# The first layer's beginning put in another order: loads, network rounds, modulation chunks, row norms, filter evacuation, angle tables

## The reference, cut to what matters

```
mod  = silu(c) @ ada_w[l] + ada_b[l]          # 6 x 1024: sh1 sc1 g1 sh2 sc2 g2
h    = rms_norm(x, ln1_g[l]) * (1 + sc1) + sh1
cols = h @ w_in[l]                            # four column groups a, b, c, d
y_d  = hyena(cols_d, filters)                 # filters: below, by FFT
x    = x + g1 * (concat(y_a, y_b, y_c, y_d) @ w_out[l])
x    = x + g2 * hier_moe(rms_norm(x, ln2_g[l]) * (1 + sc2) + sh2)

# filters: sine network of three rounds, then a product with w4 and a decay window
h = sin(f0 * (z @ w1 + b1)); h = sin(f1 * (h @ w2 + b2)); h = sin(f2 * (h @ w3 + b3))
h = (h @ w4) * window ; filt = two-sided(h) * rsqrt(sum(filt^2) + eps) ; F = rfft(filt)
# rope: cos and sin of positions * inv_freq, used by groups a, b and c
```

## Time and profile before

| | |
|---|---|
| median of three executions | 1690.1 us (1688.35 to 1690.55) |
| the profiled execution: its time | 1678.52 us |
| its span, first to last instruction | 1676.7 us |
| PE busy | 1373.4 us, 82% of the span |
| VectorE busy | 617.6 us, 37% |
| mean granted clock of TensorE | 0.929 of full |

### The profile page before, as it was taken

One profiled execution on the slowest core, in us unless ns is written; L12 is line 12 of the kernel. 1 busy time (PEld: TensorE's weight loads), 2 busy tenths in 40 slices (PEclk: granted clock), 3 DMA queues, 4 the chain that ended last, 5 costly groups with the idle time before them and its releaser, 6 DMA issues.

```text
span 1676.7 us, 18442 instructions
## 1 busy us (share of the span) xinstructions
PE 1373.4 (82%) x6748; PEld 775.2 (46%) x6748; DVE 617.6 (37%) x1444; ACT 370.6 (22%) x835; POOL 269.2 (16%) x250
## 2 busy tenths in 40 slices
PE   2779999898969589888988999998869779987731
PEld 0244655565544245444444564565544345544420
DVE  3462523256733511333153342246761432111111
ACT  0221112445521111111202112344540211111101
POOL 0000210000000053332220120000000124333211
PEclk9779999999989699999988999999989879999986
DMA  7621021267243789999943122234033669999933
GB/s 234 250 77 40 11 93 74 89 231 249 90 174 126 277 300 315 408 407 404 373 166 107 50 91 76 75 144 173 13 131 130 263 232 326 402 400 404 393 125 113
DMA packets 98608, 336.75 MB, mean 201 GB/s; under 512 B 28370, under 2 KB 33106, under 8 KB 73272
## 3 DMA queue, kind: packets, MB, share of 16 engines
q1 hardware_dynamic: 74712, 305.52, 46.7%
q0 software_dynamic: 15072, 16.85, 4.5%
q10 hardware_dynamic: 8736, 13.21, 2.2%
HBM read 324.08 MB, written 28.98 MB: 211 GB/s over the span
## 4 chain that ended last, share of the span: by engine, by line
PE 67%; DVE 14%; ACT 7%; issue 5%; DMA 3%; POOL 2%; SPq 1%; POOLq 0%; DVEq 0%; ACTq 0%
PE bank L493 62%; ACT pr_r L1333 2%; PE bank L747 2%; PE bank L842 2%; DVE pr_r L1963 2%; DVE pr_r L1822 1%; ACT pr_r L1380 1%; DVE pr_r L1966 1%; DMA big<-in_ada_w_dram 1%; DVE pr_r L1685 1%; POOL small L1451 1%; PE bank L597 1%; SPq L985 1%; ACT ht_r L1312 1%; DVE small L1820 1%
## 5 line engine op out<-in xcount | busy, mean ns | idle before, releaser
L493 PE MATMUL bank<-big,pr_r 128*64 128x256 f32 (+2 forms) x3192 | 451.8, 402 | 65.1 <-issue 25.1
L493 PEld LDWEIGHTS bank<-big,pr_r 128*64 128x64 f32 (+1 forms) x3192 | 269.3, 152 | 218.8 <-issue 108.7
L493 PE MATMUL bank<-big,ht_r 128*128 128x512 f32 (+2 forms) x832 | 330.1, 548 | 1.5 <-ACT ht_r L1346 1.5
L493 PEld LDWEIGHTS bank<-big,ht_r 128*128 128x128 f32 x832 | 155.0, 190 | 145.2 <-issue 137.6
L493 PE MATMUL bank<-big 128*128 128x256 f32 (+4 forms) x496 | 175.5, 492 | 27.9 <-ACT big L1317 10.5
L1516 POOL DMA_INDIRECT x_rows<-ht_r,slot_i x64 | 101.8, 1591 | 324.8 <-DVE ht_r L1969 289.0
L493 PEld LDWEIGHTS bank<-big 128*128 128x128 f32 (+2 forms) x496 | 94.4, 202 | 78.1 <-issue 34.2
L1963 DVE TENSOR_TENSOR pr_r<-pr_r,bank 64x256 f32<-64x256 f32 x65 | 27.5, 423 | 247.5 <-ACT pr_r L1380 236.1
L1380 ACT ACTIVATE pr_r<-bank 64x256 f32<-64x256 f32 x64 | 24.1, 377 | 408.5 <-PE bank L493 408.5
L1450 POOL TENSOR_SCALAR small<-small 128x1 f32<-128x1 f32 (+2 forms) x20 | 7.9, 396 | 561.3 <-DVE small L1847 334.0
L1969 DVE SCALAR_TENSOR_TENSOR ht_r<-bank,mix_r,mod 128x512 f32<-128x512 f32 x65 | 48.8, 751 | 132.6 <-PE bank L493 132.6
(11 more groups left out here) (296 smaller groups left out, 1254.5 us busy)
## 6 DMA issues: line engine op xcount, KB each, us to landing
big<-in_moe_w_gate_dram SPq DMA_DIRECT2D x63, 1024.0 KB, 15.7
big<-in_moe_w_up_dram SPq DMA_DIRECT2D x63, 1024.0 KB, 21.4
big<-in_moe_w_down_dram SPq DMA_DIRECT2D x63, 1024.0 KB, 23.9
big<-in_ada_w_dram SPq DMA_DIRECT2D x16, 3072.0 KB, 11.4
big<-in_w_in_dram SPq DMA_DIRECT2D x4, 3072.0 KB, 14.2
big<-in_w_out_dram SPq DMA_DIRECT2D x4, 2048.0 KB, 8.1
mod<-in_ada_b_dram SPq DMA_DIRECT2D x12, 512.0 KB, 9.9
big<-in_w_in_dram SPq DMA_DIRECT2D x2, 2048.0 KB, 8.1
```

Of the source, the lines that this page charges most:

```text
L493: return nc.tensor.matmul(o, l, r, start=start, stop=stop)
```

## The change

It puts layer 0's beginning in another order on all engines; the products and elementwise operations of the program stay the same ones.

- SyncE: `c`, the network's weights and `zT` first, then ada 0, the modulation biases, `w4` and `window`, ada 1, and only then the six other constants. Then, each when its slot or data allow: ada 2, x, the tables of waves, in d, `bias_b`, the vectors of attention, convolution and router, in a.
- PE: `f1` directly behind `f0`, `f2` behind ada 0's products, two filter row tiles ahead of ada 1's, the sums of squares further back. Of the eight DFT products the four of the cosine stay ahead of the projection, with the first transposes between them; the four of the sine go behind `d5`.
- VectorE: the three rounds without `mod_take` between them; rows of x ahead of the filters' evacuation, half of which (`fd`) goes behind the projection d; the small lambda work and the angle tables follow the evacuation of `fc`.
- ScalarE: the angle tables' sines come behind the evacuation of `hT`, as does the exponential of lambda, so its function table is loaded seven times in the program instead of five.
- Semaphores are split (`c_in`, `z_in`, `bias_in`), so that a wait names only what it needs. Scratch buffers move (`s_b_of`, `f_even_of`, `f_odd_of`, `lam_tmp`, `sq_junk`). In layer 1 the products keep their order; the lambda work goes behind its rows.

```
 @block.tensor
-            pe.wait_ge(first_load, 16 * 7)
-            pe.wait_ge(ones_set, 1)
-            pe.wait_ge(rep_ready, 1)
...
-                    pe.wait_ge(net_in, 16 * 7)
-                    pe.wait_ge(hy_in, 16 * 4)
-                    for j, (w, n) in enumerate(((hw1, 33), (hw2, 64), (hw3, 64))):
-                        if j:
-                            pe.wait_ge(mlp_ready, j)
-                        mm(V.bank(f"f{j}")[0:64, :], w, zT if j == 0 else mlp_h).then_inc(ready_v, 1)
-                        if j:
-                            mod_sum(j - 1)
-                        if j < 2:
-                            mod_parts_sum("ada", j)
...
+                    pe.wait_ge(net_in, 16 * 7)
+                    pe.wait_ge(z_in, 16)
+                    network(0)
+                    pe.wait_ge(mlp_ready, 1)
+                    network(1)
+                    pe.wait_ge(rep_ready, 1)
+                    mod_parts_sum("ada", 0)
+                    pe.wait_ge(mlp_ready, 2)
+                    network(2)
+                    pe.wait_ge(ones_set, 1)
+                    mod_sum(0)
+                    pe.wait_ge(mlp_ready, 3)
+                    pe.wait_ge(hy_in, 16 * 2)
+                    filter_rows(0)
+                    filter_rows(1)
+                    mod_parts_sum("ada", 1)
...
 @block.sync
-            load_network(0)
-            load_filters(0)
-            load_chunk(("ada", 0), 0)
-            sp.wait_ge(tables_ready, 1)
-            load_mods(0)
-            load_attention(0)
-            load_conv(0)
-            load_router(0)
-            load_chunk(("ada", 1), 0)
-            for t in range(NT):
-                sp.dma_start(x_tok[:, t, :], a["x"][0, t * P:(t + 1) * P, :]).then_inc(x_in[t], 16)
-            load_waves()
-            load_empty()
+            sp.dma_start(c_sb, a["c"].rearrange("b (p k) -> p (b k)", k=KT)).then_inc(c_in, 16)
+            load_network(0)
+            load_positions()
+            load_chunk(("ada", 0), 0)
+            load_mods(0)
+            load_filters(0)
+            load_chunk(("ada", 1), 0)
+            load_constants()
...
+                    if c == ("in", "a") and l == 0:
+                        load_bias(0)
+                        sp.wait_ge(c_ready, 1)
+                        load_attention(0)
+                        load_conv(0)
+                        load_router(0)
+                        load_empty()
 @block.scalar
-                taken(act, "fdo1")
+                act.wait_ge(nss_ready, 2 * NT * l + NT)
                 for t in range(NT):
                     evac(t)
+                act.wait_ge(lam_pre, l + 1)
+                A_(lexp, lred, ACT.Exp).then_inc(lam_exp, 1)
+                if l == 0:
+                    act.wait_ge(ang_ready, 1)
```

More of the change, by code:

```diff
@@ L554, in layer @@
                     last.then_inc(ready_v, 1)
-                    pe.wait_ge(srep_ready, l + 1)
+                    mod_sum(2)
+                    pe.wait_ge(first_load, 16 * 6)
+                    pe.wait_ge(srep_ready, 1)
                     b = V.bank("fnb")
@@ L1634, in mod_take @@
                         took(last)
-                if l == 0:
-                    v.wait_ge(net_in, 16 * 7)
-                    v.wait_ge(hy_in, 16 * 4)
-                    step(TS(bias_b, bias_b, 2.0 / (2 * S), None, ALU.mult))
-                    for j in range(3):
-                        b = V.take(f"f{j}")
-                        took(TS(mlp_y, b[0:64, :], hb[:, j:j + 1], hf[:, j:j + 1], ALU.add, ALU.mult))
-                        reduce_angle(step, mlp_y, mlp_k).then_inc(sin_in, 1)
-                        if j:
-                            v.wait_ge(mod_in, 16 * 4)
-                            mod_take(j - 1)
-                else:
+                if l:
                     v.wait_ge(mod_in, 16 * 4 * (l + 1))
@@ L1693, in rows, with filter_evac @@
                         last.then_inc(hrow_ready, 1)
-                if l == 0:
+                def filter_evac(kind):
+                    dst = {"c": fc, "d": fd}[kind]
+                    even, odd, scale = f_even_of[l], f_odd_of[l], s_b_of[l]
+                    for m in range(2):
+                        b = V.take(f"f{kind}e{m}")
+                        took(TT(even, b[:, :], scale, ALU.mult))
+                        if kind == "c":
+                            step(TT(even, even, bias_b, ALU.add))
+                        b = V.take(f"f{kind}o{m}")
+                        took(TT(odd, b[:, :], scale, ALU.mult))
+                        TT(dst[:, m, 0], even, odd, ALU.add)
+                        step(TT(dst[:, m, 1], even, odd, ALU.subtract))
@@ L1710, in layer @@
-                for t in range(0 if l else 2, NT):
-                    if t >= 2:
-                        done(v, f"hT{t - 2}1")
-                    rows(t, gsc1, sh1)
+                for t in range(2, NT):
+                    done(v, f"hT{t - 2}1")
+                    rows(t, gsc1, sh1)
+                if l == 0:
+                    v.wait_ge(bias_in, 16)
+                    step(TS(bias_b, bias_b, 2.0 / (2 * S), None, ALU.mult))
+                    filter_evac("c")
+                v.wait_ge(vec_in, 16 * 12 * (l + 1))
```

213 lines of the change are left out of this document (120 added, 93 removed).

## The result

| | before | after |
|---|---|---|
| median | 1689.22 us (1681.28 to 1690.55, 4 executions) | 1643.53 us (1640.46 to 1648.56, 4 executions) |
| profiled execution: time | 1678.52 us | 1640.46 us |
| its span | 1676.7 us | 1638.6 us |
| mean granted clock | 0.929 | 0.938 |
| PE busy | 1373.4 us | 1363.1 us |

The change is faster: ratio 0.9748, 95% interval 0.9725 to 0.9772. The medians lie 45.7 us apart, the two profiled executions 38.1, since the one of before was quick for its kernel.

The account below looks back on a forecast made before the run. Until projection d at 116.94 load and engine waits bound the kernel, then PE's products. Gains of 27.1 and 14.8 (41.9), minus 7.0 handed back, plus 2.3 for clock, gave 37.2: median 1653 us, range 1644 to 1667.

Parts of the forecast that it names:

- First part: Program start until the third sine: reordered loads and an earlier third round end it at 29.0 instead of 56.1, gaining 27.1.
- From 29.0 to `fn`: PE's filter rows, ada 1's products, sums of squares and ada 2's products, forecast to run from 29.0 to 55.6.
- Rival 2: The order works, but PE runs at half clock or ada 1 is late: gain 21 to 32, chance 0.27.
- From `fnb` to the projection: PE's cosine products and transposes beside VectorE's rows: from 58.6, last rows released by transposes, projection d at 75.
- Handed back: The four sine groups, moved behind `d5` where PE is the bound, cost 7.0 of the gain.
- At nothing: Filter evacuation, tables, late vectors, in d, layer 1's lambda work and two more function table loads: covered, costing nothing.
- limit of HBM: A cited page's 358 GB/s for one core would bring ada 1 some 4 us later and cut the gain by that.
- rival 1: The forecast itself: whole kernel gains 32 to 43 us, chance 0.60.
- rival 3: Better than forecast: chunks' products take less than 4.3 and ada 0 comes at 17.3; gain 43 to 47, chance 0.07.
- three signs of failure: Ada 1's products after 40, clock at 0.50 from 30 to 60, or PE waiting for banks inside the projection.
- Rival 4: Slower: late vectors hold ScalarE's first convolution step and the d banks, each us past 102 costing one; chance 0.03.
- Rival 5: The gained time ends at once in another wait, as an in d landing at 115; time 1690, chance 0.03.

Follow-up runs that it names:

- e2: Changed kernel with the third network round behind ada 1's products again, on all engines; median 1658.83 us, ratio 0.9831 to the kernel before.
- e5: Changed kernel plus seven products nobody reads, between `mod_sum(0)` and the filter rows, where PE idled; median 1642.94 us, ratio 0.9717 to before.
- e1: Changed kernel with SyncE's order of loads as before, other engines in the new order; median 1657.49 us, ratio 0.9805 to the kernel before.
- e11: The changed kernel, unedited, measured a third time; median 1647.06 us, ratio 0.9742 to the kernel before.
- e4: Changed kernel with the four sine groups between the last transposes and the projection, filters evacuated in one go; median 1643.94 us, ratio 0.9726 to before.
- e3: Changed kernel with all filter evacuation ahead of rows 2 and 3, and sine groups ahead of the projection, as before; median 1648.42 us, ratio 0.9767.
- e10: Changed kernel with split modulation loads, seven unread products, a halved scale product and second transposes moved; median 1641.04 us, ratio 0.9707 to before.
- e0: The changed kernel, unedited, measured again; median 1646.55 us, ratio 0.9744 to the kernel before.
- e9: Changed kernel with the third modulation bias and `ln1` loaded behind ada 1, with their own semaphore; median 1646.43 us, ratio 0.9744 to before.
- e6: Changed kernel with unread products: seven ahead of `f0`, nine behind it, seven behind `mod_sum(0)`; median 1640.96 us, ratio 0.9706 to before.

## Why the prediction was right

By its own steps, forecast and measured in the changed kernel:

| step | forecast | measured |
|---|---|---|
| `f0` | 8.5 | 7.71 |
| ada 0's products | 18.5, 4.24 long | 17.47, 5.35 long |
| third sine done | 29.0 | 29.0 |
| ada 1's products | 33.2 to 37.5 | 35.33 to 40.5; the chunk landed at 34.2 in e2, 34.4 in e5 |
| ada 2 issued; its products | 23; no wait | 30.09; no wait |
| `fnb` | 58.6 | 58.25 |
| projection d | 75 | 72.53 |
| sine groups handed back | -7.0 | -7.03 |
| projection shorter | +2.3 | +3.04 |
| group a, earlier by | 37.2 | 40.6 |
| experts, earlier by | 37.2 | 43.2 |

**First part.** 27.1 us as forecast. e1 and e2 undo one cause each, and each brings back its own wait: at group a the loads cost 11, the third round's place 15. No run undid both. That the third sine came at 29.0 to the tenth is luck in part: the loads came 1.0 earlier than forecast, and the products of ada 0 took 1.1 longer (5.35; 4.63 in e11). The granted clock reads 1.00 in those stretches, so no row shows why.

**From 29.0 to `fn`.** Rival 2 was partly there. The filter rows took 6.33 for the 3.6 forecast and ada 1's products 5.2 for 4.3. But only some 10 us ran at half clock (30 to 40, by the granted clock) instead of half of 35, and what these products lost was mostly time in which ada 1 was still under way: e5 keeps the clock at 1.00 in the filter rows and gains 1.7 at group a. The steps behind were over-sized: 12.8 forecast for rows, sums and `mod_sum`, 9.1 measured from 40.44 to 49.5. The sum products of tiles 0 and 1 (x8) took 1.92 in one row, where I had counted 3.8, and tile 3's went in between ada 2's products. The errors cancelled, which is luck: `fnb` was forecast at 58.6 and came at 58.25.

**From `fnb` to the projection.** This is the term that was mis-sized, by 2.1 us: forecast 16.4, measured 14.3. The chain was the forecast one, rows 3 freed by PE's transposes (68.04, after an idle time of 0.54 that PE ended), but `fnb` took 1.13 for the 2.07 assumed and the last transposes 1.16 for 1.97; both prices came from stretches of the trace of before with a granted 0.69 (84 to 88) and 0.50 (112 to 116), and after the change the clock was 1.00 in both places.

**Handed back.** 7.03, and e4 shows that it is the price of the products and not of their place. e3 shows what the rows' place buys, with this paid: 8.5 at group a.

**At nothing.** All held as a price, one of them for another reason than forecast. SyncE's queue was late by 7 for ada 2 and by some 11 for the vectors, as issues take 4 to 6 us while chunks are queued; both had cover. The angle tables' block ended at 84.1. ScalarE's table loads: 

```profile
72.49 1.28 ACT L1273 ACT_TABLE_LOAD   x1
78.49 0.20 ACT L1273 ACTIVATE small<-small 128x2 f32<-128x2 f32 x1 [4.71 <-DVE small L1734]
78.71 1.28 ACT L1277 ACT_TABLE_LOAD   x1
...
277.77 1.28 ACT L1367 ACT_TABLE_LOAD   x1 [2.93 <-DVE small L1853]
279.07 0.69 ACT L1367 ACTIVATE pr_r<-bank,small 128x512 f32<-128x512 f32 x1
```

The first follows the last evacuation of `hT` at once and ends 4.7 us before its work; the one for the first softmax was forecast to lie inside ScalarE's wait, and did not. It starts only behind the wait of 2.93 (2.95 in the earlier trace rows, without a load) and puts the first softmax operation off by 1.3. The rows show no cost for PE even so: before, ScalarE idled another 0.93 and 0.61 between its next operations, and no longer did. From the end of the first VectorE reduction to PE's next products with the probabilities (x8) 4.51 passed before and 4.28 after. The Trainium skill, page "ScalarE: Activation LUTs", section "What ACT_TABLE_LOAD costs", puts 2.66 us to a switch, 1.38 of them a drain; the 1.28 of the load agrees with these rows, and no drain shows in them.

**The 6 us beyond the forecast.** 2.5 are the projection's start and 0.7 its clock, which with rounding makes 40.6 at group a for 37.2. The other 2.6 came between group a and the experts: PE's products there had 0.96 of the clock in 160 to 200 after the change, and 0.91 in the matching 200 to 240 before; 0.95 in 400 to 440, and 0.93 in 440 to 480 before. In 240 to 280, against 280 to 320 before, it was the other way, 0.91 and 0.93. The edits do not reach there, apart from the table load above. e10 lost 3.1 in the same stretch. So the stretch moves by some 3 us either way, perhaps with where idle moments fall; that the clock is all of it was not shown. The measured 43.7 on average (e0, e11) is then the experts' 43.2.

On the limit of HBM: the stretches 28 to 32 and 36 to 44 show 402 to 408 GB/s (301 in the one between), so the 358 of the page that the prediction named does not hold here. The Trainium skill, page "Perfetto Trace Analysis", section "Roofline", says for a single active core that it can pull more, up to about 435 GB/s; these rows agree with that, and by it ada 1's estimate needs no extra 4 us.

**Rivals.** By size the profiled pair (38.1) is in rival 1 (32 to 43), the average of three comparisons (43.7) and the first (45.7) are in rival 3 (43 to 47), which had a chance of 0.07. Rival 3's way was only half there: ada 0's products began at 17.47, as it says, but the chunks' products took 5.35 and 5.18, not less than 4.3. None of the three signs of failure occurred: ada 1's products at 35.33, a granted 0.50 only up to about 40, no wait inside the projection. Rival 4 (late vectors) was not near: the last was issued by 66, and VectorE's first convolution step ran at 84.14, behind the tables, 18 ahead of the 102 from which it would have counted. Rival 5 did not occur.

## What to carry to other kernels

At a program's start, walk each wait back to the load or product that it really needs: a semaphore shared by four loads held the first product back by 6.2 us here (what that alone costs the kernel was not shown), and loads out of the order of their use cost 11. Move the work that only a late consumer reads (tables, filters' evacuation) behind the start of the long block of products, and count what PE work comes along: it is handed back one for one. Two small improvements can hide behind each other (the filler, an earlier chunk): only together did they bring ada 1's products to 32.88. But follow such a gain to the end: e10 stood 4.1 us ahead of e5 at group a, 0.4 behind it at the experts, and had the same ratio.

## What the runs showed of the hardware

- An issue by SyncE that took 0.42 to 0.6 us in an empty queue took 4.09 (a chunk) with one chunk of 3 MB and all the biases ahead, and 6.32 (positions) and 9.43 (a bias, in e9) with two chunks ahead. Issues further down slip by it: ada 2's went out at 30.09 for the 23 forecast. How much has to be queued for it was not measured; e9's ada 1, issued at 9.07 behind one chunk, two biases, `w4` and `window`, took 0.58.
- After a wait of 3.6 us filter rows ran at a granted 0.50; with seven unread products (x14) in that wait they ran at 1.00, in 3.70 us instead of 6.33. The gain was mostly lost at the next wait, for a load.
- Gains at group a did not arrive at the experts as they were: e5 and e6 stood 1.7 and 1.4 ahead and then 3.1 and 2.9, e10 5.8 and then 2.7, with the same program in between. The granted clock in single stretches was the difference seen (0.50 and 0.67 where the same products, x28, took 9.17 and 8.00).
